# A two-block transformer kernel on one core: throwaway products of TensorE taken out of all its waits but the first

## The chip, the cores and the metric

The kernel runs on one NeuronCore of a Trainium2 chip, in float32. The core has TensorE (matrix products; PE in the profile, with its weight loads apart as PEld), VectorE (DVE), ScalarE (ACT), GpSimd (POOL) and SyncE (SP, which here only starts transfers). They run side by side and wait for each other by semaphores. The metric is the device time of one execution in microseconds (us). Three executions of the kernel before took 2404.06, 2407.88 and 2408.59 us; the median is 2407.88.

## The reference

Two blocks of two layers each work on 256 tokens of 1024 numbers. Cut to what matters here:

```
# first block, for each of 2 layers
h = rms_norm(x, norm_gain[layer]);  proj = h @ w_in[layer]
... sparse attention and a gated delta rule on parts of proj, mixed by gates ...
x = x + mixed @ w_out[layer]
x = rms_norm(x, final_gain)
# second block, for each of 2 layers
a = rms_norm(h, norm_attn[i]);  u = a @ w_in[i]
... four mixers on parts of u ...
h = h + mix @ w_out[i]
c = rms_norm(h, norm_ffn[i])
h = h + (swiglu(c) if i == 0 else moe_swiglu(c))      # moe: top 2 of 8 experts
gate = sigmoid(rms_norm(h, ple_norm[i]) @ ple_w_gate[i])
h = h + (p[i] @ ple_w_proj[i]) * gate
```

The routing of the second layer is

```
logits = x @ router;  top_val, top_idx = top_k(logits, 2);  top_w = softmax(top_val)
out = sum over experts e of combine[:, e] * swiglu_e(x)
```

## The kernel before, in words

The 256 tokens stand as two tiles of 128 partitions. The residual X stays in SBUF, and weights stream in over SyncE's queue into a ring. Every product is in float32, which TensorE runs as two passes: where this text says "three products", the trace counts six.

Before each large product X is normalised. There are nine such norms, n = 0 to 8; norm 2, the end of the first block, is taken together with norm 3. TensorE's part in a norm is `norm_pe`: it turns half of X (four blocks of 128 columns, two token tiles, line 474) into PSUM, from where VectorE writes it, times the gain, to HT (line 597). This is done for the left half of X first, then for the right. A half can be turned once the residual's sum is in X, which VectorE says by `x_updated` (`xf_ready` for norm 3). The left half is often turned in the middle of the last product of the stage before. `norm_rest_pe` (line 660) does the right half, which comes when that product has ended, and so TensorE has nothing of its own to do until VectorE has added the last 512 columns to X.

In this wait the kernel before puts throwaway products. `keep_busy(bank, times)` (line 640) multiplies the identity with one of its own columns, spread to 256, into a PSUM bank that nobody reads then. It waits for nothing but what stands ahead of it in TensorE's order. It is called at twelve places: four products ahead of the first input (line 3626), three in each of the seven `norm_rest_pe` but that of norm 8, three behind `setup_pe`, which turns the small parameters (lines 3419 and 3421) once at the start, four behind the router's logits (line 2862), two ahead of the first experts' gather (line 3038) and two behind it (line 3043).

The order on each engine is the order of the code; where stages overlap, plans written as tables say after how many steps of one another's steps stand. No plan holds a throwaway product.

At the start, the stage is: identity ready; four throwaway products; left half of X turned; three; right half turned; parameters turned; three; then the first product of layer 0 (line 683, lhs HT, first weights in the ring). Its k-th step waits for the k-th block of HT.

In the second layer of the second block the route goes: router logits (line 2859, 32 passes of 8 columns), the top two by VectorE (lines 2875 to 2882), four small products that count places (lines 2864 to 2867), the first experts' places by VectorE (lines 2885 to 2926), the gather of their tokens as products (line 3020, 32 passes), its way out of PSUM by VectorE (line 3232), and then the experts' wide products (line 2968) and down products (line 2981), all eight experts one behind another.

Of the kernel before, what the change touches and what calls it, by code (L numbers as in the profile page):

```python
# [66 lines left out]
def blocks_kernel(nc, A, out):  # L67
    ctx = ExitStack()
    with ctx:
        sems = {}  # L70

        def sem(name):
            if name not in sems:
                sems[name] = ctx.enter_context(nc.semaphore(name))
            return sems[name]
# [20 lines left out]
        def signal(name):  # L96
            return sem(CHAINED[name][0] if name in CHAINED else name)

        def reached(name, times):

            if name in CHAINED:
                _, i, n = CHAINED[name]
                return n * (times - 1) + i + 1
            return times
# [360 lines left out]
        def ht_lhs(k, t):  # L465
            return HT[:, k, t * P:(t + 1) * P]
# [11 lines left out]
        def bc(ap, shape):  # L478
            return ap.to_broadcast(shape)
# [104 lines left out]
        def fresh_from(n):  # L584

            m = turned(n)
            return 2 * KD * min(m, DEPTH) + KD * max(0, m - DEPTH)
# [52 lines left out]
        def keep_busy(bank, times):  # L640

            for _ in range(times):
                nc.tensor.matmul(PS[:, bank, 0:S], IDENT, bc(IDENT[:, 0:1], [P, S]), start=True, stop=True)

        def idle_bank(n):

            return {0: 3, 1: 2, 3: 2}.get(n, 0)

        def norm_pe(pe, n, half):

            if n == DEPTH + 1:
                pe.wait_ge(sem("xf_ready"), half + 1)
                src = XGAIN
            else:
                x_half(pe, n, half)
                src = X
            blocks = [(lambda t, k=k: src[:, t, k * P:(k + 1) * P]) for k in range(4 * half, 4 * half + 4)]
            transposes(blocks, 4 + 2 * half).then_inc(sem("norm_transposed"), 1)

        def norm_rest_pe(pe, n):  # L660
            if n != 8:
                keep_busy(idle_bank(n), 3)
            norm_pe(pe, n, 1)
            if n == 0:
                setup_pe(pe)
                keep_busy(3, 3)

        U = view(0, T * (QKV0)).rearrange("p (t c) -> p t c", t=T)
# [1982 lines left out]
        def ple_turn_pe(pe, L, bank):  # L2652
            pe.wait_ge(sem("ple_loaded"), 16 * (L + 1))
            transposes([(lambda t, j=j: PP[:, t, j * P:(j + 1) * P]) for j in range(2)], bank).then_inc(sem("ple_T"), 1)
# [126 lines left out]
        def half_places(t):  # L2781

            return slice(HALF_CAP * t, HALF_CAP * t + HALF_CAP)
# [12 lines left out]
        def group_places(g, t):  # L2796

            return WSEL[:, t].rearrange("p e s -> p (e s)")[:, g * P:(g + 1) * P]
# [53 lines left out]
        def ms(name):  # L2852
            return sem("moe_" + name)

        def route_pe(pe, n):
            for k in range(KD):
                pe.wait_ge(sem("ht_ready"), fresh_from(n) + (k + 1))
                for t in range(T):
                    last = nc.tensor.matmul(PS[:, 2 * t, 0:NE], ht_lhs(k, t), ROUTER[:, k, :],
                                            start=k == 0, stop=k == KD - 1)  # L2860
            last.then_inc(signal("moe_logits"), 1)
            keep_busy(7, 4)
            pe.wait_ge(signal("moe_mask"), reached("moe_mask", 1))
            nc.tensor.matmul(PS[:, 5, 0:NE], SUPPER, MASK[:, 0, :], start=True, stop=True)
            nc.tensor.matmul(PS[:, 5, NE:2 * NE], SUPPER, MASK[:, 1, :], start=True, stop=True)
            nc.tensor.matmul(PS[:, 5, 2 * NE:3 * NE], ONES, MASK[:, 0, :], start=True, stop=True)
            nc.tensor.matmul(PS[:, 5, 3 * NE:4 * NE], ONES, MASK[:, 1, :], start=True, stop=True)\
                .then_inc(signal("moe_places"), 1)
# [144 lines left out]
        def first_pe(pe):  # L3013

            def gather(i, half):
                for k in range(4 * half, 4 * half + 4):
                    c = k % 2 * 2 * CAP
                    for t in range(T):
                        two = PS[:, (6, 3)[half] + k % 4 // 2, c:c + 2 * CAP].rearrange("p (a s) -> p a s", a=2)
                        last = nc.tensor.matmul(two[:, :, half_places(t)], XN[:, t, k * P:(k + 1) * P],  # L3020
                                                PALL[:, t, 2 * i:2 * i + 2, :], start=True, stop=True)
                last.then_inc(ms("gather"), 1)

            def scatter(i, bank=6):
                g, t = SCATTERS[i]
                for dh in range(2):
                    last = nc.tensor.matmul(PS[:, bank + dh, :], PWG[:, g, t * P:(t + 1) * P],  # L3027
                                            YTG[g % 3][:, 512 * dh:512 * dh + 512], start=True, stop=True)
                last.then_inc(ms("scatter"), 1)

            def weights_turned(g0, g1):
                for g in range(g0, g1):
                    for t in range(T):
                        last = nc.tensor.transpose(PS[:, 6 + (g - g0) // 2, g % 2 * S + t * P:g % 2 * S + (t + 1) * P],
                                                   group_places(g, t), IDENT)
                last.then_inc(ms("placedT"), 1)

            keep_busy(4, 2)
            pe.wait_ge(ms("placed"), 1)
            pe.wait_ge(signal("moe_tokens"), reached("moe_tokens", 1))  # L3040
            gather(0, 0)
            gather(0, 1)
            keep_busy(0, 2)
            for e in range(NE):
                n = SCATTER_AT.get(e)

                def tokens(k, b):
                    c = CAP * (e % 2) + 32 * b
                    return XGP[:, k, c:c + 32]

                if e % 2 == 0:
                    pe.wait_ge(ms("XG"), e + 2)
                wide(pe, 0, e, 0, 0, 3, tokens)
                if e == 0:
                    pe.wait_ge(ms("weighed"), 1)
                    weights_turned(0, 4)
                elif n is not None:
                    pe.wait_ge(ms("YT"), e)
                    if n:
                        pe.wait_ge(ms("added"), n)  # L3060
                    scatter(n)
                wide(pe, 0, e, 0, 3, 6, tokens)
                if n is not None and e % 2:
                    pe.wait_ge(ms("added"), n + 1)
                    scatter(n + 1)
                wide(pe, 0, e, 0, 6, 8, tokens)
                wide(pe, 0, e, 1, 0, 8, tokens)
                if e == 0:
                    pe.wait_ge(ms("PWT"), 1)
                    weights_turned(4, 6)  # L3070
                elif e % 2 == 0 and n is not None:
                    pe.wait_ge(ms("added"), n + 1)
                    scatter(n + 1)
                elif e == 1:
                    pe.wait_ge(ms("PWT"), 2)
                elif n is not None:
                    pe.wait_ge(ms("added"), n + 2)
                if e == NE - 1:
                    ple_turn_pe(pe, 1, 7)
                elif e % 2:  # L3080
                    gather((e + 1) // 2, 0)
                    pe.wait_ge(ms("h"), 2 * e + 2)
                    gather((e + 1) // 2, 1)
                down(pe, 0, e, 0, 24)
                down_last(pe, 0, e)
            pe.wait_ge(sem("ple_pT"), 2)
            ple_unit(pe, 1, 0, 0, 3).then_inc(sem("ple_unit"), 1)
            pe.wait_ge(ms("YT"), NE)
            scatter(len(SCATTERS) - 2)
            scatter(len(SCATTERS) - 1, 4)  # L3090
            ple_unit(pe, 1, 0, 1, 0).then_inc(sem("weights_used"), 1)
# [325 lines left out]
        def setup_pe(pe):  # L3417
            pe.wait_ge(sem("col_params"), 16 * N_COLS)
            nc.tensor.transpose(PS[:, 0, 0:64], PSTAGE[0:64, 0, :], IDENT[0:64, 0:64])
            for L in range(DEPTH):  # L3420
                last = nc.tensor.transpose(PS[:, 0, 64 + 96 * L:160 + 96 * L], PSTAGE[0:96, 1 + L, :],
                                           IDENT[0:96, 0:96])
            last.then_inc(sem("param_cols_T"), 1)
# [266 lines left out]
```

## Time and profile before

| | |
|---|---|
| median of three executions | 2407.88 us |
| the profiled execution, its own time | 2409.21 us |
| span of its trace | 2407.4 us |
| TensorE busy | 2354.6 us, 98% |
| VectorE busy | 821.1 us, 34% |
| ScalarE busy | 462.9 us, 19% |
| transfers | 542.56 MB, mean 225 GB/s |
| experts' stage | 1462 to 2380 us, TensorE busy 914.51 us of 918 |

The profiled execution's own time is 1.8 us above its span; what lies outside the span is ahead of the first and behind the last instruction of the core. It is 1.3 us above the median.
### The profile page before, as it was taken

The numbers are of one execution on the slowest core, as the hardware profiler recorded it, in microseconds if no ns is written. First come the engines' busy times: TensorE is split into PE (matmuls) and PEld (weight loads), VectorE is DVE, ScalarE is ACT, GpSimd is POOL, SyncE is SP. The second block draws the span as 40 slices with busy tenths as digits, with TensorE's granted clock in tenths as the row PEclk, the third lists the DMA queues.
The fourth block names the chain that finished last, engine by engine and source line by source line (L and its number), as shares of the span: only waits on it lengthen the run. The fifth ranks groups of instructions, "written<-read, shape, count | busy, mean of one in ns | idle before, by whom it ended". The sixth has DMA issues, their size and how long they took to land. (4 is left out here: it accounts for less than half of the span.)

```text
span 2407.4 us, 51252 instructions
## 1 busy us (share of the span) xinstructions
PE 2354.6 (98%) x23229; PEld 1364.4 (57%) x23229; DVE 821.1 (34%) x1665; ACT 462.9 (19%) x794; POOL 139.7 (6%) x356
## 2 busy tenths in 40 slices
PE   9999999999999999999999899999999999999999
PEld 8755557855555676997455654435343534343444
DVE  3545623444543554666635531101010101101012
ACT  1532321432323542000025431000000000000001
POOL 5011000011000310000003100000000000000000
PEclk9999999999999999999999999999999999999999
DMA  7522334432335513445446128999999999999992
GB/s 246 168 89 72 122 123 140 137 108 79 104 100 148 176 55 120 154 169 183 158 133 187 52 93 342 397 402 378 405 397 409 379 387 399 369 384 396 388 369 97
DMA packets 194447, 542.56 MB, mean 225 GB/s; under 512 B 29200, under 2 KB 61360, under 8 KB 194224
## 3 DMA queue, kind: packets, MB, share of 16 engines
q1 hardware_dynamic: 180576, 536.82, 60.8%
q8 instruction: 185, 3.03, 0.5%
q10 hardware_dynamic: 13344, 1.35, 0.5%
q0 software_dynamic: 304, 1.05, 0.1%
q14 instruction: 38, 0.31, 0.0%
HBM read 538.12 MB, written 1.05 MB: 224 GB/s over the span
## 5 line engine op out<-in xcount | busy, mean ns | idle before, releaser
L407 PE MATMUL psum<-ring,hT 128*128 128x512 f32 (+3 forms) x1120 | 478.4, 576 | 6.0 <-ACT area L831 4.5
L2968 PE MATMUL psum<-ring,mix 128*32 128x448 f32 x4608 | 438.5, 539 | 0.7 <-DVE mix L3232 0.7
L407 PEld LDWEIGHTS psum<-ring,hT 128*128 128x128 f32 x1120 | 206.0, 190 | 206.4 <-issue 180.9
L2968 PEld LDWEIGHTS psum<-ring,mix 128*32 128x32 f32 x4608 | 148.8, 110 | 282.9 <-issue 280.7
L3221 DVE TENSOR_TENSOR area<-area,psum 128x1344 f32<-128x1344 f32 x16 | 24.6, 1535 | 470.6 <-PE psum L2968 470.6
L712 PE MATMUL psum<-hT,ring 128*128 128x256 f32 x768 | 166.4, 379 | 0.0
L712 PEld LDWEIGHTS psum<-hT,ring 128*128 128x128 f32 x768 | 145.9, 190 | 20.7 <-issue 1.0
L2981 PE MATMUL psum<-area 128*32 128x256 f32 x2688 | 148.2, 379 | 1.9 <-DVE area L3223 1.9
L2968 PE MATMUL psum<-area,mix 128*32 128x448 f32 x1536 | 147.2, 539 | 0.0
L2981 PE MATMUL psum<-ring,area 128*32 128x256 f32 x2688 | 146.5, 379 | 0.0
L2981 PEld LDWEIGHTS psum<-area 128*32 128x32 f32 x2688 | 86.5, 110 | 61.4 <-DVE area L3223 3.2
L2981 PEld LDWEIGHTS psum<-ring,area 128*32 128x32 f32 x2688 | 87.3, 110 | 57.8
L3165 ACT ACTIVATE area<-psum 128x256 f32<-128x256 f32 x24 | 9.2, 384 | 512.1 <-PE psum L2981 512.1
L1699 PE MATMUL psum<-ring,hT 128*128 128x256 f32 x384 | 102.8, 413 | 1.2 <-ACT area L1627 1.2
L2968 PEld LDWEIGHTS psum<-area,mix 128*32 128x32 f32 x1536 | 49.9, 110 | 94.4 <-issue 94.4
L3259 DVE COPY hT<-area 32x256 f32<-32x256 f32 x64 | 18.2, 285 | 223.6 <-ACT area L3165 222.9
L1699 PEld LDWEIGHTS psum<-ring,hT 128*128 128x128 f32 x384 | 73.4, 202 | 19.0 <-issue 5.7
L3157 ACT ACTIVATE area<-psum 128x1344 f32<-128x1344 f32 x16 | 20.7, 1291 | 272.2 <-PE psum L2968 272.2
L2446 PE MATMUL psum<-area 128*128 128x128 f32 x576 | 66.3, 275 | 0.0
L2446 PEld LDWEIGHTS psum<-area 128*128 128x128 f32 x576 | 65.3, 192 | 0.0
L1517 PE MATMUL psum<-ring,hT 128*128 128x512 f32 x128 | 59.5, 623 | 4.0 <-issue 4.0
L920 DVE SCALAR_TENSOR_TENSOR area<-area,param_cols 128x256 f32<-128x256 f32 x144 | 60.5, 482 | 1.3
(592 smaller groups left out, 2581.5 us busy)
## 6 DMA issues: line engine op xcount, KB each, us to landing
ring<-in_w_in_dram SPq DMA_DIRECT2D x88, 1024.0 KB, 5.1
ring<-in_moe_w_gate_dram SPq DMA_DIRECT2D x96, 896.0 KB, 7.0
ring<-in_moe_w_up_dram SPq DMA_DIRECT2D x96, 896.0 KB, 8.0
area<-in_moe_w_down_dram SPq DMA_DIRECT2D x112, 512.0 KB, 5.9
ring<-in_moe_w_down_dram SPq DMA_DIRECT2D x112, 512.0 KB, 6.5
area<-in_moe_w_gate_dram SPq DMA_DIRECT2D x32, 896.0 KB, 7.3
area<-in_moe_w_up_dram SPq DMA_DIRECT2D x32, 896.0 KB, 7.6
ring<-in_w_out_dram SPq DMA_DIRECT2D x16, 1024.0 KB, 5.0
```

Of the source, the lines that this page charges most:

```text
L407: last = nc.tensor.matmul(acc(g)[:, t, 0:d["n"]], lhs(kk, t), w[:, k, :], start=kk == 0, stop=kk == d["nk"] - 1)
L712: last = nc.tensor.matmul(acc(g)[:, j // 2, (j % 2) * S:(j % 2) * S + S], half_view(n, (4, 512))[:, k % 4, j * P:(j + 1) * P], HT[:, k, :] ...
L920: ins = nc.vector.scalar_tensor_tensor(Y[:, c, :], XC[:, c, tap:tap + S], w, Y[:, c, :], ALU.mult, ALU.add)
L1517: last = nc.tensor.matmul(acc(g)[:, t, :], mixed(k)[:, 4 * h + kk, t * P:(t + 1) * P], w[:, kk, :], start=h + kk == 0, stop=h == 1 and kk ...
L1699: last = nc.tensor.matmul(acc(g)[:, t, :], ht_lhs(k, t), w[:, k, :], start=k == 0, stop=k == KD - 1)
L2446: last = nc.tensor.matmul(out[:, j, :], w[:, k, j * P:(j + 1) * P], h[:, k, :], start=k == 0, stop=k == 3)
L2968: last = nc.tensor.matmul(PS[32 * j:32 * j + 32, 3 * p + b, 0:PIECE].rearrange("p (m n) -> p m n", n=32), tokens(k, b), w[:, :, j, :], sta ...
L2981: return nc.tensor.matmul(PS[32 * jj:32 * jj + 32, b, 0:256], HET[:, i // 14, b, 32 * (i % 14):32 * (i % 14) + 32], ring_cols(chunk_place( ...
L3157: nc.scalar.activation(HE[:, p], PS[:, 3 * p:3 * p + 3, 0:PIECE], ACT.Silu).then_inc(ms("sg"), 1)
L3165: nc.scalar.activation(YE[:, b, :], PS[:, b, 0:256], ACT.Copy).then_inc(ms("YE"), 1)
L3221: nc.vector.tensor_tensor(HE[:, p], HE[:, p], PS[:, 3 * p:3 * p + 3, 0:PIECE], ALU.mult).then_inc(ms("h"), 1)
L3259: ins = nc.vector.tensor_copy(YTG[g % 3][r0:r0 + 32, 256 * j:256 * j + 256], YE[32 * j:32 * j + 32, b, :])
```

## The change

All calls of `keep_busy` are taken out but the one ahead of the first input (line 3626). Thirty-two products, 64 passes, go from eleven places. No other instruction is added or moved; a semaphore wait that stood on a throwaway product goes to the instruction behind it.

```diff
         def norm_rest_pe(pe, n):
-            if n != 8:
-                keep_busy(idle_bank(n), 3)
             norm_pe(pe, n, 1)
             if n == 0:
                 setup_pe(pe)
-                keep_busy(3, 3)
...
             last.then_inc(signal("moe_logits"), 1)
-            keep_busy(7, 4)
             pe.wait_ge(signal("moe_mask"), reached("moe_mask", 1))
...
-            keep_busy(4, 2)
             pe.wait_ge(ms("placed"), 1)
             pe.wait_ge(signal("moe_tokens"), reached("moe_tokens", 1))
             gather(0, 0)
             gather(0, 1)
-            keep_busy(0, 2)
             for e in range(NE):
```

TensorE's order around norm 5, the one ahead of the gate product of the second block's first layer, before (L474 turns the right half of X, L2666 are the products of the per-layer input, L407 is the gate product):

```order
L2666 MATMUL psum<-ring,area 128x512 [waits landed0,ple_pT]
L2666 MATMUL psum<-ring,area 128x512
L643 MATMUL psum<-ident 128x256 [waits ple_out_dve]
L643 MATMUL psum<-ident 128x256 x2
L474 MATMUL psum<-ident,x 128x128 [waits x_updated]
L474 MATMUL psum<-ident,x 128x128 x7
L2666 MATMUL psum<-ring,area 128x512 [waits landed0]
L2666 MATMUL psum<-ring,area 128x512
L407 MATMUL psum<-ring,hT 128x512 [waits ht_ready,landed1,x_updated]
```

The same place now (the lines have moved by three):

```order
L2663 MATMUL psum<-ring,area 128x512 [waits landed0,ple_pT]
L2663 MATMUL psum<-ring,area 128x512
L474 MATMUL psum<-ident,x 128x128 [waits x_updated,ple_out_dve]
L474 MATMUL psum<-ident,x 128x128 x7
L2663 MATMUL psum<-ring,area 128x512 [waits landed0]
L2663 MATMUL psum<-ring,area 128x512
L407 MATMUL psum<-ring,hT 128x512 [waits ht_ready,landed1,x_updated]
```

The wait for `ple_out_dve`, VectorE's copy of the first of these products, stood on the first throwaway product and stands on the turning now.

TensorE's order from the end of the router's logits to the first expert, before (the small products are L2864 to L2867, the gather is L3020, the first expert L2968):

```order
L2859 MATMUL psum<-router,hT 128x8
L643 MATMUL psum<-ident 128x256 x4
L2864 MATMUL psum<-area,supper 128x8 [waits route_by_vector]
L2865 MATMUL psum<-area,supper 128x8
L2866 MATMUL psum<-area,ones 128x8
L2867 MATMUL psum<-area,ones 128x8
L643 MATMUL psum<-ident 128x256 x2
L3020 MATMUL psum<-area,xn 128x2x48 [waits route_by_scalar,moe_placed]
L3020 MATMUL psum<-area,xn 128x2x48 x15
L643 MATMUL psum<-ident 128x256 x2
L2968 MATMUL psum<-ring,mix 32x448 [waits moe_landed1,moe_XG]
```

And now:

```order
L2856 MATMUL psum<-router,hT 128x8
L2860 MATMUL psum<-area,supper 128x8 [waits route_by_vector]
L2861 MATMUL psum<-area,supper 128x8
L2862 MATMUL psum<-area,ones 128x8
L2863 MATMUL psum<-area,ones 128x8
L3016 MATMUL psum<-area,xn 128x2x48 [waits route_by_scalar,moe_placed]
L3016 MATMUL psum<-area,xn 128x2x48 x15
L2964 MATMUL psum<-ring,mix 32x448 [waits moe_landed1,moe_XG]
```

Eight products are gone from three waits that lie within ten microseconds; the real products stand as they stood.

## Rows read from the trace of the kernel before

**Rows 1.** The page, the chain that ended last, shares of the span by line.
```profile
PE psum L2968 23%; PE psum L2981 12%; PE psum L1517 1%; PE psum L1699 1%; PE psum L3027 1%; DVE area L3221 1%; PE psum L407 1%; PE psum L2690 1%; PE psum L474 0%; ACT area L2027 0%; PE psum L2666 0%; PE psum L2012 0%; PE psum L3020 0%; DVE area L3223 0%; PE psum L1988 0%
```

**Rows 2.** Timeline of TensorE, norm 5: start us, us, what, idle before it.
```profile
1214.93 1.57 PE L643 MATMUL psum<-ident 128*128 128x256 f32 x6 [0.85 <-DVE mix L2643]
1216.34 1.03 PE L474 MATMUL psum<-ident,x 128*128 128x128 f32 x8
```

**Rows 3.** Timeline of VectorE and of TensorE, norm 6.
```profile
1250.83 0.69 DVE L2729 TENSOR_TENSOR x<-x,area 128x512 f32<-128x512 f32 x1
...
1252.02 1.04 PE L474 MATMUL psum<-ident,x 128*128 128x128 f32 x8
```

**Rows 4.** Timeline of TensorE, norm 1, whose wait is that of norms 4 and 7.
```profile
374.13 3.60 PE L1517 MATMUL psum<-ring,area 128*128 128x512 f32 x8
...
379.12 1.09 PE L474 MATMUL psum<-ident,x 128*128 128x128 f32 x8
```

**Rows 5.** Timeline of TensorE, norm 3.
```profile
747.97 1.47 PE L643 MATMUL psum<-ident 128*128 128x256 f32 x6
750.78 1.09 PE L474 MATMUL psum<-ident,mix 128*128 128x128 f32 x8 [1.34 <-DVE mix L551]
```

**Rows 6.** Timeline of TensorE, the start.
```profile
6.60 1.47 PE L643 MATMUL psum<-ident 128*128 128x256 f32 x6
7.91 1.04 PE L474 MATMUL psum<-ident,x 128*128 128x128 f32 x8
9.15 0.27 PE L3419 MATMUL psum<-ident,area 64*128 64x64 f32 x1 [0.20 <-DMA area<-in_conv_w_dram]
...
9.57 1.50 PE L643 MATMUL psum<-ident 128*128 128x256 f32 x6
11.60 4.56 PE L683 MATMUL psum<-ring,hT 128*128 128x256 f32 x20 [0.53 <-DVE hT L597]
16.07 0.71 PE L688 MATMUL psum<-ident,small 128*128 128x128 f32 x4
```

**Rows 7.** Timeline of TensorE, and of VectorE at 1459.60, the route.
```profile
1448.21 3.64 PE L2859 MATMUL psum<-router,hT 128*128 128x8 f32 x32
...
1453.89 0.39 PE L2864 MATMUL psum<-area,supper 128*128 128x8 f32 x2 [0.20 <-DVE area L2882]
...
1454.81 1.11 PE L643 MATMUL psum<-ident 128*128 128x256 f32 x4
1456.09 3.81 PE L3020 MATMUL psum<-area,xn 128*128 128x96 f32 x32 [0.16 <-DVE area L2926]
...
1459.60 1.82 DVE L3232 TENSOR_TENSOR mix<-psum,param_cols 128x768 f32<-128x768 f32 x2
...
1461.48 0.96 PE L2968 MATMUL psum<-ring,mix 128*32 128x448 f32 x8 [0.69 <-DVE mix L3232]
```

**Rows 8.** Timeline of TensorE, waits without throwaway products elsewhere.
```profile
841.44 1.14 PE L1988 MATMUL psum<-area 64*128 64x256 f32 x8 [1.59 <-DVE mix L1926]
...
861.40 1.93 PE L2012 MATMUL psum<-area 128*32 128x64 f32 x64 [2.12 <-ACT area L2035]
...
910.46 8.80 PE L1517 MATMUL psum<-ring,hT 128*128 128x512 f32 x16 [1.99 <-issue]
...
1338.61 1.09 PE L2001 MATMUL psum<-ident,area 128*128 128x128 f32 x8 [2.75 <-ACT area L2027]
```

**Rows 9.** Stretches behind those waits: engines' busy us, granted clock (PEclk), transfers.
```profile
841.40:844.90 3.50, 3.46 (x77) 2.62 (x78) 2.15 (x2) 0.61 (x2) 0.00 (x0) 1.00 0.02 5
859.70:866.40 6.70, 5.00 (x71) 4.22 (x72) 2.94 (x8) 3.36 (x8) 4.66 (x10) 0.50 0.03 8
910.80:914.20 3.40, 3.40 (x5) 1.35 (x4) 1.59 (x3) 1.07 (x2) 0.00 (x0) 0.50 0.00 0
1340.90:1344.30 3.40, 2.67 (x7) 1.59 (x5) 2.19 (x4) 2.80 (x4) 0.00 (x0) 0.50 0.00 0
```

**Rows 10.** Timeline of TensorE, the same 64 passes as at 861.40, at full clock.
```profile
1346.59 1.10 PE L2012 MATMUL psum<-area 128*32 128x64 f32 x64
```

## The prediction

> **What bounds the kernel now.** I read the page first. The chain that ended last runs nearly wholly over TensorE's products [rows 1], those of the experts ahead of all, and TensorE has no long pause in any slice. A microsecond won or lost on TensorE ahead of the experts therefore goes to the end, where nothing else covers it. The second view is the timeline at the eleven places. For each the question is what ended the wait in which the throwaway products stood. If real work behind them started when they ended, they delayed it. If it started later, with idle time of its own, taking them out wins nothing, and the wait is then wholly idle. The third view is the granted clock behind such idle waits elsewhere in this trace. A product at 1.2 GHz takes twice its time, and this is what the change can cost.
>
> **What is won.** A throwaway set of three products is six passes. Six take 1.47 us with a tail of 0.16 [rows 5], so they stand 0.215 us apart and hold TensorE for 1.3 us.
>
> Norm 5: the throwaway passes start at 1214.93, where VectorE's copy ends, and the turning starts at 1216.34, with no idle time between [rows 2]. The right half of X had long been there, since VectorE adds it ahead of that copy. Now the turning starts at 1214.93. A turning that was waited for takes 1.09 us against 1.04 for one that was not [rows 4, 2], so the gain is 1216.34 - 1214.93 - 0.05 = 1.36 us. Behind it stand real products that wait for nothing late; the gate product needs the right half's first block of HT only after its first sixteen passes. All 1.36 us should come through.
>
> Norm 6: VectorE's sum of the right half ends at 1250.83 + 0.69 = 1251.52, and the turning starts at 1252.02 [rows 3]. With 0.04 us for the semaphore it could start at 1251.56. The gain is 0.46, less the same 0.05: 0.4 us.
>
> Norms 1, 4 and 7 look alike: the real product ends at 374.13 + 3.60 = 377.73, and the turning starts at 379.12, after the throwaway passes, when VectorE's sum has ended [rows 4]. Nothing is won, and the idle wait is 1.39 us. Norm 3: the turning waits 1.34 us beyond the throwaway passes for VectorE [rows 5]. Nothing is won.
>
> The start: the right half is turned at 7.91, and could be at about 6.6. But the parameters that are turned next are waited for until 9.15, by a transfer, and the first product at 11.60 waits for VectorE's HT, which hangs on the parameters [rows 6]. Nothing is won. The route: the small products wait for VectorE at 1453.89, the gather for VectorE at 1456.09, the first expert for VectorE at 1461.48, each with idle time of its own [rows 7]. Nothing is won by the eight products there.
>
> The sum of gains is 1.36 + 0.4 = 1.8 us. It could be 1.3 if norm 6 gives nothing and 2.0 at most; nothing else of the 64 passes stands in the way of work.
>
> **What it can cost.** The trace shows four idle waits of TensorE without throwaway products. Behind 1.59 us at 841.44 the clock stays at 1.00. Behind 2.12, 1.99 and 2.75 us it goes to 0.50, for 6.7 us once and 3.4 us twice [rows 8, 9]. Each wait of the changed kernel is set beside the nearest of these four. The price: 16 wide passes behind the wait at 910.46 take 8.80 us [rows 8]. Eight at full clock take 3.60 [rows 4], so 16 take 2 x 3.44 + 0.16 = 7.04. One fall onto wide products costs 1.76 us. Small passes lose too: the same 64 take 1.93 us at half clock and 1.10 at full [rows 8, 10], a factor of 1.75.
>
> Now the waits as they become.
>
> Norms 1, 4, 7: 1.39 us idle with dense work on both sides. Shorter than 1.59, so no fall: 0. The other end is 1.76 each.
>
> Norm 3: the last real pass ends about 747.97 + 0.16, the turning starts at 750.78 [rows 5]: 2.65 us idle. By the row of 2.75 it falls. The half stretch may begin during the wait, and then part of it lies on nothing. Between 0 and 1.76; I take 1.2, since it may also not fall at all in some executions.
>
> The start: the right half's turning would end at about 7.6, then 1.5 us idle until 9.15, half a microsecond of small turnings, whose tail ends at 9.57 + 0.16 = 9.73, and from there to 11.60 idle again, 1.87 us [rows 6]. The two together are longer than any of the waits that fell. The half clock then lies on the first product, whose 20 passes run from 11.60; they end at 11.60 + 20 x 0.215 = 15.9, and the next group waits for VectorE until 16.07, which covers 0.17. One stretch of 3.4 us costs up to 1.76 - 0.17 = 1.6, and one of 6.7 us, as at 859.70, 3.2. The least is 0. I take 1.3.
>
> The route: from the logits' end at 1448.21 + 3.64 = 1451.85 to 1453.89 TensorE idles 2.04 us; then eight small passes until 1454.81 + 0.16 = 1454.97, and 1.12 us idle to the gather at 1456.09 [rows 7]. A fall is nearly certain. It lies on the eight small passes (1.08 us, at 1.75 times 0.8 more) and on the gather (3.81 us, up to 2.9 more). A stretch of 3.4 us wholly on the gather loses 3.4 x (1 - 1/1.75) = 1.45. VectorE's second instruction of L3232 starts at 1459.60 + 0.91 = 1460.51 [rows 7], 0.6 us after the gather's end, and covers so much: 0.85 left. One that begins at the small passes gives 0.8 + 0.2. A long stretch gives up to 2.4. Between 0 and 2.4; I take 1.2.
>
> The first expert: 1459.90 to 1461.48, 1.58 us idle behind a gather of light passes [rows 7]. It is just at the row that held, so a fall is as likely not: between 0 and 1.76; I take 0.4.
>
> The sum: -1.8 + 1.3 + 1.2 + 1.2 + 0.4 = +2.3 us. On the profiled execution's own 2409.21 that is 2411.5. This execution is 1.3 us above the median of the runs, so for the median I forecast 2410.2.
>
> The ends: all gains and no fall gives -1.8 to -2.0. All falls at their dearest gives 3.2 + 1.76 + 2.4 + 1.76 - 1.8 = +7.3, and three more at the quiet norms +12.6.
>
> **A rule that speaks against the change.** The trace shows turnings at full clock: eight passes in 1.04 us [rows 2, 3, 6]. Whether the chip counts them as work when it decides on the clock, no row here says alone. The Trainium skill, "TensorE: Matmul & The Clock Gate", section "Part 4: PE-mode transpose", says that the full clock "doesn't engage" for transposes, since they don't count as busy in the same way. By this the pause at norms 1, 4 and 7 would be longer for the chip than the 1.39 us of the row, and these would fall too. It is the second rival.
>
> **The rivals.** A change within 0.2% (4.8 us) is what a measurement of this kernel can't tell from none; the three runs spread over 4.5 us.
>
> First rival: the clock does not fall at the new waits, because the work around them is denser than around those that fell. For it: 1.59 us held, and each of norms 1, 4, 7 is shorter. Against it: norm 3's 2.65 us and the two pairs at the start and in the route are as long as those that fell or longer. Then only the gains stay: 2407.88 - 1.8 = 2406.1. Chance 0.17.
>
> Second rival: turnings don't hold the clock, and norms 1, 4 and 7 fall too. A turning's 0.9 us adds to 1.39 and makes 2.3 us, beyond the 1.99 that fell. The stretch lies on the wide product behind, 1.3 to 1.76 us each, so 4 to 5.3 more: 2414.2 to 2415.5. For it: nothing in the rows excludes it. Against it: the wait before 841.44 is as long as these and held, though no turning stands beside it. Chance 0.1.
>
> Third rival, the slower one: the half clock lasts a second stretch, because what stands behind the wait is itself sparse. The places are the start, where the first product is only begun when the stretch is half over, and the route, where small passes and another wait follow. The row of 6.7 us at 0.50 shows that it happens: its work was sparse, busy 5.00 us of it by a view that counts tails [rows 9]. Price: 3.2 at the start and 2.4 in the route in place of 1.3 and 1.2, with norm 3 and the first expert at 1.76: +7.3, so 2415.2. It decides the sign of the measurement from a total loss of 6.6 us on. Chance 0.23.
>
> The forecast keeps 0.5: two to four falls of single stretches, 2407.5 to 2413.
>
> **How the numbers follow.** Slower by over 0.2% is above 2412.7: a tenth of the forecast's 0.5, most of the second rival and nearly all of the third, 0.05 + 0.08 + 0.2 = 0.33. Faster by over 0.2% is below 2403.1, for which no term is large enough; 0.04 is left for the spread of the runs beside the first rival. Within 0.2% is the rest, 0.63. The range is 2405.5 to 2416: it takes in the first rival and the third, and leaves out the second at full price.
>
> **What would show it.** The turning at norm 5 starts right at VectorE's copy, 1.4 us earlier against its neighbours; at norm 6 it starts at VectorE's sum. The waits at norms 1, 3, 4 and 7 end where they end now. The granted clock stands at 0.50 behind norm 3, in the first 16 us and between 1453 and 1461, and the first product's 20 passes take 5 to 6 us in place of 4.56. If the clock is 1.00 there, the first rival holds; if 0.50 stands behind norms 1, 4 and 7, the second; if it lasts more than 4 us at the start or in the route, the third. The forecast is wrong if the experts' stage changes in length, since no term of it touches that.

## The result, and the profile after

The changed kernel takes 2414.61 us in the median of 16 executions (2406.24 to 2425.01), the kernel before 2409.66 in 16 (2404.06 to 2412.72). The ratio is 1.0024, with a 95% interval of 1.0013 to 1.0036: 3 to 9 us slower. The forecast was 2410.2, with 2405.5 to 2416 as its range and +2.3 us as its sum, and it gave a time within 0.2% the larger chance, 0.63 against 0.33 for slower; what came lies just outside. The sign was right, and the size was half of what came. The losses stand at the places named, and at one more that the forecast did not have.

The profiled execution of the changed kernel took 2410.15 us, the second fastest of its sixteen. So the two traces can't be set against each other by their ends, only place by place. Between the places both kernels have stretches in which the clock falls in one execution and not in the next. From 380 to 743 us, for one, the two traces drift by 2.5 us against each other, with no changed instruction there.

In the trace before, the clock stood at 1.00 at the start, at norm 3 and in the route. The rows are stretches: engines' busy us (PE, PEld, DVE, ACT, POOL), then the granted clock, the share of the transfers and GB/s.

```profile
9.70:13.12 3.42, 2.89 (x14) 2.25 (x13) 3.24 (x8) 0.00 (x0) 3.15 (x5) 1.00 0.98 334
13.12:16.53 3.41, 3.41 (x19) 2.78 (x18) 2.40 (x9) 0.20 (x1) 2.84 (x10) 1.00 1.05 399
...
750.39:753.81 3.42, 3.03 (x18) 2.68 (x19) 2.82 (x8) 1.36 (x4) 0.00 (x0) 1.00 0.51 172
...
1446.00:1462.00 16.00, 14.87 (x110) 12.65 (x112) 11.77 (x41) 4.72 (x7) 0.75 (x1) 1.00 0.90 361
```

The same places in the changed kernel, with norms 1 and 4. They answer to [rows 9], which had only waits elsewhere.

```profile
11.30:18.10 6.80, 5.72 (x14) 4.59 (x15) 5.03 (x15) 0.20 (x1) 5.78 (x17) 0.50 1.04 389
...
383.00:386.40 3.40, 3.17 (x19) 2.92 (x20) 2.77 (x9) 0.72 (x2) 0.00 (x0) 1.00 0.86 304
...
752.10:755.40 3.30, 3.02 (x11) 2.78 (x12) 1.86 (x6) 1.26 (x4) 0.00 (x0) 0.50 0.45 153
...
945.00:948.40 3.40, 3.20 (x19) 2.95 (x20) 2.77 (x9) 0.72 (x2) 0.77 (x1) 1.00 0.99 347
...
1448.40:1458.50 10.10, 7.13 (x33) 7.04 (x33) 6.76 (x30) 2.94 (x4) 0.00 (x0) 0.50 0.94 389
```

The reader is to see the clock column: 1.2 GHz at the start for 6.8 us, behind norm 3 for 3.4, and in the route for 10.1. Behind norms 1 (383) and 4 (945) it stays at 2.4 GHz.

What it did to the work stands in the timeline of TensorE, the start first. It answers to [rows 6].

```profile
6.76 1.09 PE L474 MATMUL psum<-ident,x 128*128 128x128 f32 x8 [0.35 <-DMA x<-in_x_dram]
9.93 0.27 PE L3413 MATMUL psum<-ident,area 64*128 64x64 f32 x1 [2.07 <-DMA area<-in_conv_w_dram]
...
12.38 7.40 PE L680 MATMUL psum<-ring,hT 128*128 128x256 f32 x20 [1.86 <-DVE hT L597]
19.61 0.61 PE L685 MATMUL psum<-ident,small 128*128 128x128 f32 x4
```

The 20 passes of the first product take 7.40 us, where they took 4.56. The parameters' transfer also landed later, at 9.93 instead of 9.15; that has nothing to do with the change, as the traces of the kernels below show, where the first product starts 0.3 to 1.3 us later than in the trace before, with and without the throwaway products at the start. From the first pass of this product to the first of the next one (line 709, 712 before) it is 2.66 us more.

Norms 3, 5 and 6, which answer to [rows 5], [rows 2] and [rows 3], in the timeline of TensorE:

```profile
752.38 1.97 PE L474 MATMUL psum<-ident,mix 128*128 128x128 f32 x8 [2.64 <-DVE mix L551]
...
1215.45 1.09 PE L474 MATMUL psum<-ident,x 128*128 128x128 f32 x8 [0.85 <-DVE mix L2640]
...
1250.74 1.09 PE L474 MATMUL psum<-ident,x 128*128 128x128 f32 x8 [0.70 <-DVE x L2726]
```

At norm 3 even the turning runs at half clock, 1.97 us instead of 1.09. At norms 5 and 6 the turning follows VectorE at once.

The route, which answers to [rows 7]:

```profile
1443.62 1.09 PE L474 MATMUL psum<-ident,x 128*128 128x128 f32 x8 [1.38 <-DVE x L1548]
1444.55 3.64 PE L2856 MATMUL psum<-router,hT 128*128 128x8 f32 x32
1450.23 0.60 PE L2860 MATMUL psum<-area,supper 128*128 128x8 f32 x2 [2.04 <-DVE area L2878]
...
1453.25 6.34 PE L3016 MATMUL psum<-area,xn 128*128 128x96 f32 x32 [1.14 <-DVE area L2922]
1460.63 1.71 PE L2964 MATMUL psum<-ring,mix 128*32 128x448 f32 x16 [1.05 <-DVE mix L3226]
```

The gather takes 6.34 us instead of 3.81. The clock fell at 1448.33, when the logits had only just ended at 1448.19 (1444.55 + 3.64): the passes of 8 columns had kept TensorE at work until then, with no pause since 1443.62.

The experts' stage, which the prediction named as the part that must not change, did not: from its first pass to the first of the four products ahead of norm 8's turning it is 908.05 us before and 908.04 now.

Behind it, at norm 8, stands one thing that no term of the sum had. No throwaway product ever stood there:

```profile
2370.51 0.87 PE L474 MATMUL psum<-ident,x 128*128 128x128 f32 x6
2372.89 1.31 PE L474 MATMUL psum<-ident,x 128*128 128x128 f32 x10 [1.51 <-issue]
```

The same in the trace of the kernel before:

```profile
2371.36 1.97 PE L474 MATMUL psum<-ident,x 128*128 128x128 f32 x16
```

After six of sixteen passes TensorE stands for 1.51 us, and the profile shows nothing that it waits for (`issue`).

### The profile page after: what moved, and what is told of

Read it like the earlier page. It is cut to its first block, busy times and chain, and to the rows that moved or that the text cites. A ratio compares the mean times of both kernels' runs of the same rounds, so it can differ in the third digit from the quotient of the medians.

```text
span 2408.3 us, 51125 instructions
## 1 busy us (share of the span) xinstructions
PE 2341.5 (97%) x23165; PEld 1356.5 (56%) x23165; DVE 820.9 (34%) x1665; ACT 462.9 (19%) x794; POOL 138.4 (6%) x356
## 3 DMA queue, kind: packets, MB, share of 16 engines
q10 hardware_dynamic: 13344, 1.35, 0.5%
## 4 chain that ended last, share of the span: by engine, by line
PE 61%; DVE 2%; issue 1%; ACT 1%; DVEq 0%; ACTq 0%
PE psum L2964 23%; PE psum L2977 12%; PE psum L2443 6%; PE psum L407 4%; PE psum L2478 3%; PE psum L1696 3%; PE psum L1514 2%; PE psum L2424 1%; PE psum L3023 1%; PE psum L474 1%; DVE area L3215 1%; PE psum L2687 1%; PE psum L2663 1%; PE psum L3016 1%; PE psum L2259 0%
## 5 line engine op out<-in xcount | busy, mean ns | idle before, releaser
L407 PE MATMUL psum<-ring,hT 128*128 128x512 f32 (+3 forms) x1120 | 477.6, 575 | 7.0 <-ACT area L828 4.5
L407 PEld LDWEIGHTS psum<-ring,hT 128*128 128x128 f32 x1120 | 206.3, 191 | 207.6 <-issue 182.0
```

What stands on the lines that cost most here:

```text
L407: last = nc.tensor.matmul(acc(g)[:, t, 0:d["n"]], lhs(kk, t), w[:, k, :], start=kk == 0, stop=kk == d["nk"] - 1)
```

## The experiments

All kernels are the kernel before with the edits shown, cut to what matters. Behind each stand the medians of its executions and of the kernel before beside it, and the ratio on record with its 95% interval. That ratio is not the quotient of the two medians and lies up to 0.0008 from it. The table gives what a place costs in each trace: the start of a pass behind the place minus the start of a pass ahead of it, less the same in the trace before (the starts as the timelines have them). The places are the start (first pass of the first product to the first of the next), norm 3 (743 to 756 us), norms 5 and 6 (1209 to 1218.9, and 1249.8 to 1257), the route (first pass of the logits to the experts' first) and norm 8 (2369.5 to 2374.9).

| kernel | start | norm 3 | norm 5 | norm 6 | route | norm 8 |
|---|---|---|---|---|---|---|
| changed | +2.66 | +1.46 | -1.35 | -0.38 | +2.81 | +1.73 |
| changed, again | +2.09 | +1.67 | -1.35 | -0.39 | +4.30 | +1.82 |
| e8_after147 | +1.85 | +1.67 | -1.35 | -0.39 | +3.05 | 0 |
| e1_start | +2.58 | 0 | 0 | 0 | 0 | 0 |
| e2_norm3 | +0.11 | +1.68 | 0 | 0 | +1.87 | 0 |
| e3_route | +0.10 | 0 | 0 | 0 | +2.86 | 0 |
| e4_norm56 | +0.10 | 0 | -1.35 | -0.38 | 0 | 0 |
| e5_norm147 | +0.12 | 0 | 0 | 0 | +2.83 | 0 |
| e7_mix | +0.11 | 0 | -1.35 | -0.38 | +3.52 | 0 |
| e10_mix_ffn | +0.11 | 0 | -1.35 | -0.39 | +1.86 | 0 |
| e11_light | +1.89 | 0 | 0 | 0 | +3.52 | 0 |
| e12_light_again | +1.50 | 0 | 0 | 0 | +3.52 | 0 |
| e13_light_third | +1.46 | 0 | 0 | 0 | +3.52 | 0 |

**e1_start: the start alone.**

```diff
         def norm_rest_pe(pe, n):
-            if n != 8:
+            if n in (1, 3, 4, 5, 6, 7):
                 keep_busy(idle_bank(n), 3)
...
                 setup_pe(pe)
-                keep_busy(3, 3)
```

> Only the six products at the start are taken out (three ahead of the right half's turning in norm 0, three behind the parameters). Clock theory: the granted clock falls to 0.50 ahead of or in the first product of layer 0, and stays there for 3.4 or 6.8 us; the first product's 20 passes take 6 to 8 us in place of 4.56, and the run is 1.5 to 3.3 us slower than before. Rival (the cost is code placement: TensorE stood 1.5 us for no shown reason in the turning of norm 8 in the changed kernel): the start costs nothing, and the time follows whether that stop appears in norm 8.

Measured: 2409.0 us against 2406.91, ratio 1.0008 (0.9996 to 1.0020), not told from no change by its time. The trace shows the mechanism, timeline and clock:

```profile
11.99 7.33 PE L682 MATMUL psum<-ring,hT 128*128 128x256 f32 x20 [1.86 <-DVE hT L597]
```

```profile
10.90:17.60 6.70, 5.61 (x13) 4.55 (x14) 5.03 (x15) 0.20 (x1) 5.63 (x18) 0.50 1.05 389
```

6.8 us at half clock again, 2.58 us lost. The code placement rival is out for this place: the loss is there, and norm 8 is unchanged.

**e2_norm3: norm 3 alone.** `if n in (0, 1, 4, 5, 6, 7):` ahead of the call.

> Only the three products ahead of norm 3's right half are taken out. Clock theory: 0.50 for 3.4 us around the turning or the product behind it, 1.0 to 1.7 us slower than before. Rival (code placement): clock and time as before at norm 3; any loss shows as a stop of TensorE in norm 8.

Measured: 2406.04 against 2406.91, ratio 1.0001 (0.9990 to 1.0013): the loss of 1.0 to 1.7 us is not to be seen in the times. In the trace norm 3 costs 1.68 us:

```profile
749.40:752.70 3.30, 3.30 (x9) 2.34 (x9) 2.69 (x11) 0.21 (x1) 0.00 (x0) 0.50 0.00 0
1445.70:1452.40 6.70, 6.70 (x25) 5.88 (x24) 3.84 (x21) 2.46 (x3) 0.00 (x0) 0.50 1.02 428
```

The second row is a surprise: the clock fell in the route too, with all its throwaway products in place.

**e3_route: the route alone.** The three calls `keep_busy(7, 4)`, `keep_busy(4, 2)` and `keep_busy(0, 2)` are out.

> Only the eight products of the route are taken out (behind the logits, ahead of and behind the first gather). Clock theory: the clock falls in the route, and the stretch from the logits' end to the first expert's first wide pass grows by 2 to 3.5 us over the 9.6 us of before; the run is 2 to 3.5 us slower. Rival (code placement): this stretch grows by less than 0.5 us.

Measured: 2409.31 against 2406.91, ratio 1.0007 (0.9994 to 1.0020), not told from no change. In the trace the route costs 2.86 us, with 10.2 us at half clock:

```profile
1441.40:1451.50 10.10, 7.28 (x33) 7.19 (x34) 6.61 (x30) 2.78 (x4) 0.00 (x0) 0.50 0.91 381
```

**e4_norm56: norms 5 and 6 alone.** `if n in (0, 1, 3, 4, 7):` ahead of the call.

> Only the products ahead of the right halves of norms 5 and 6 are taken out. Here they delayed work: the turning of norm 5 should start at VectorE's copy, 1.4 us earlier, and that of norm 6 0.4 us earlier, with the clock at 1.00 there; 1.8 us faster than before. Rival (the clock falls here too): 0 to 1.5 us slower.

Measured: 2403.26 against 2406.91, ratio 0.9986 (0.9975 to 0.9997): faster. The two gains are there to a tenth, 1.35 and 0.38 us, and the clock stays up at both:

```profile
1213.36 1.09 PE L474 MATMUL psum<-ident,x 128*128 128x128 f32 x8 [0.85 <-DVE mix L2643]
...
1248.65 1.09 PE L474 MATMUL psum<-ident,x 128*128 128x128 f32 x8 [0.70 <-DVE x L2729]
```

```profile
1209.00:1218.00 9.00, 8.15 (x31) 4.37 (x31) 6.41 (x16) 2.85 (x8) 0.00 (x0) 1.00 0.52 137
1244.00:1254.00 10.00, 9.30 (x44) 6.60 (x43) 7.27 (x17) 4.97 (x11) 0.00 (x0) 1.00 0.59 186
```

**e5_norm147: norms 1, 4 and 7 alone.** `if n in (0, 3, 5, 6):` ahead of the call.

> Only the products ahead of the right halves of norms 1, 4 and 7 are taken out, where the waits become 1.4 us of idle time. Theory: each of the three turnings starts where it did, the clock stays at 1.00 behind norms 1 and 4, and the run is within 1 us of before; at norm 7 the logits with their light passes follow, and the clock may fall there more often than before. Rival (turnings don't hold the clock): 0.50 behind norms 1 and 4 too, 1.3 to 1.8 us each, 4 to 5 us slower in all.

Measured: 2407.99 against 2406.09, ratio 1.0000 (0.9990 to 1.0010). Norms 1 and 4 cost nothing, and the clock is at 1.00 behind both, so the rival is refuted there. Norm 7 is another matter: the clock fell in the logits behind it.

```profile
1444.86 1.09 PE L474 MATMUL psum<-ident,x 128*128 128x128 f32 x8 [1.38 <-DVE x L1551]
1445.79 5.39 PE L2859 MATMUL psum<-router,hT 128*128 128x8 f32 x32
1451.04 3.53 PE L643 MATMUL psum<-ident 128*128 128x256 f32 x8
```

The logits take 5.39 us instead of 3.64, and the route costs 2.83. This is one trace. In e7_mix below the clock fell in the logits too, with norm 7's products in place.

**e8_after147: the changed kernel with norms 1, 4 and 7 put back.** `if n in (1, 4, 7): keep_busy(idle_bank(n), 3)`, all other calls as in the changed kernel.

> The changed kernel with the three products of norms 1, 4 and 7 put back, 36 instructions of TensorE more than the changed kernel and 92 fewer than before, all ahead of the branch behind the experts. Code placement theory: the stop of 1.5 us in the turning of norm 8 goes away, and the run is 1 to 2 us faster than the changed kernel, 3 to 4 slower than before. Rival (the stop belongs to something else, or to chance): it stays or varies, and the time is that of the changed kernel.

Measured: 2412.46 against 2406.09, ratio 1.0020 (1.0010 to 1.0031). The stop in norm 8 is gone:

```profile
2375.74 1.97 PE L474 MATMUL psum<-ident,x 128*128 128x128 f32 x16
```

The other places cost about what they cost in the changed kernel. But the times do not show the 1 to 2 us that were expected back: 1.0020 (1.0010 to 1.0031) here and 1.0024 (1.0013 to 1.0036) for the changed kernel are not told apart.

**The changed kernel again.**

> The changed kernel once more. Code placement theory: the stop of 1.5 us in the turning of norm 8, after its first six passes, stands in this trace at the same pass. The clock falls again at the start, at norm 3 and in the route, the lengths of the stretches can differ. Chance theory: the stop is gone or elsewhere.

Measured: one execution, 2412.14 us. The stop is there, at the same pass (the view ends at 2376 us):

```profile
2372.51 0.88 PE L474 MATMUL psum<-ident,x 128*128 128x128 f32 x6
2374.99 1.20 PE L474 MATMUL psum<-ident,x 128*128 128x128 f32 x9 [1.60 <-issue]
```

The clock fell at all three places again, in the route for 13.7 us (4.30 us lost).

**e7_mix: norms 5 and 6 out, and throwaway products where the clock fell before.**

```diff
             gemm_begin(pe, left)
+            if k >= DEPTH:
+                keep_busy(TILES[left]["bank"], 4)
             pe.wait_ge(sem("mixT_ready"), 2 * k + 1)
```

> The products ahead of norms 5 and 6 are taken out, as in e4_norm56, and four products each are put into the two waits of TensorE between the turning of the first half of the mixers' output and the output product (2 us of idle time, in both layers of the second block), into the bank that the product fills next. Theory: the clock no longer falls at about 910 and 1410 us, each of which costs up to 1.76 us in the executions where it falls; 0.5 to 3 us faster than e4_norm56, 3 to 6 us faster than before. Rival (the throwaway products delay the product, or the fall comes elsewhere): as e4_norm56 or slower.

Measured: 2401.46 against 2406.09 in seven executions, ratio 0.9977 (0.9963 to 0.9990): faster than the kernel before. From e4_norm56, with 0.9986 (0.9975 to 0.9997), it is not told apart by its time. The output product's 16 passes, 8.80 us in [rows 8], take 7.13 in both layers:

```profile
910.82 1.91 PE L643 MATMUL psum<-ident 128*128 128x256 f32 x8
912.93 7.13 PE L1517 MATMUL psum<-ring,hT 128*128 128x512 f32 x16 [0.20 <-ACT hT L1543]
```

At these two waits the clock fell behind 14 of 24 in the twelve traces without products there, and behind none of the four in this trace and e10_mix_ffn's.

In this trace, too, the clock fell in the route, for 10.2 us, in spite of the products there. It fell at 1442.42, in the middle of the logits, which started at 1439.53 and take 4.20 us; ahead of them norm 7's products and turning stand with no pause.

**e10_mix_ffn: one more place.** As e7_mix, with `keep_busy(7, 4)` ahead of `ple_turn_pe(pe, L, 7)` in the dense layer.

> e7_mix, and four more throwaway products in the dense layer's down product, ahead of the turning of the per-layer input, where TensorE then waits 2.2 us for VectorE's sums (the clock fell there, at about 1197 us, in most traces). Theory: no fall there, 1 to 1.8 us less in the executions where it fell: 0 to 1.8 us faster than e7_mix. Rival (the four products hold up the turning, whose output is needed later): as e7_mix or up to 1.7 us slower.

Measured: 2403.38 against 2407.65, ratio 0.9978 (0.9964 to 0.9992). The clock doesn't fall at 1197 us, but it didn't there in e7_mix either, nor in e3_route and the changed kernel, which have no products there. So one trace doesn't show that the products did it, and by its time the kernel is not told apart from e7_mix.

**e11_light: light throwaway products at the start and in the route.** In short (the line `keep_light(3, 6)` stands twice in the kernel, ahead of norm 0's turning and behind `setup_pe`):

```diff
+        def keep_light(bank, times):
+            for _ in range(times):
+                nc.tensor.matmul(PS[:, bank, 0:8], IDENT, bc(IDENT[:, 0:1], [P, 8]), start=True, stop=True)
...
-                keep_busy(3, 3)
+                keep_light(3, 6)
...
-            keep_busy(7, 4)
+            keep_light(7, 8)
...
-            keep_busy(4, 2)
+            keep_light(4, 4)
...
-            keep_busy(0, 2)
+            keep_light(0, 4)
```

> The products at the start and in the route stand where they stood, but are of 8 columns in place of 256, and twice as many: 6, 6, 8, 4 and 4 products of about 0.22 us each, so that TensorE is as long at work by the trace. Theory A (the kind of work counts, as the fall during the router's 8-column logits suggests): the clock falls at the start and in the route as if nothing stood there; first weights' product 20 passes in 6 to 7.4 us, route 2 to 3 us longer, run 4 to 6 us slower than before. Theory B (being busy is enough): no fall at the start, and the time of before within 1 us.

> The kernel of e11_light once more, for a second trace. In its first trace the clock fell at the start and in the route, but that execution was the slowest of its ten. If passes of 8 columns don't hold the clock (theory A), it falls at both places again: 0.50 in the first product of layer 0, whose 20 passes take 6 us or more, and in the route. If it depends on the execution (theory C), one of the two is at 1.00, with 4.56 us for the 20 passes.

> The same kernel a third time, the same question: theory A has the clock fall at both places again, theory C at one or none.

The clock fell at both places in all three traces. The first one's, stretches and timeline:

```profile
10.30:17.00 6.70, 6.70 (x24) 5.89 (x23) 5.85 (x15) 0.20 (x1) 5.81 (x15) 0.50 1.01 373
1454.20:1464.30 10.10, 10.10 (x49) 10.10 (x49) 6.15 (x27) 2.24 (x3) 0.00 (x0) 0.50 0.85 358
```

```profile
10.38 2.62 PE L648 MATMUL psum<-ident 128*128 128x8 f32 x12
12.85 6.63 PE L690 MATMUL psum<-ring,hT 128*128 128x256 f32 x20
```

TensorE is busy for all of the 10.10 us, and stands at half clock. The start decides between the theories: with products of 256 columns there the clock fell in none of seven traces, with products of 8 columns in three of three. The route alone would not, since the clock fell there in three of six traces with the wide products too.

But by its times the kernel is not 4 to 6 us slower: 2408.46 against 2407.65 in ten executions, ratio 1.0000 (0.9986 to 1.0014), at most 3.4 us. Their mean granted clock is lower, 0.9893 against 0.9908. The three traced executions took 2414.20, 2416.94 and 2412.58. Theory A holds for what the traces show; why the timed executions lose less stays open.

## Why the prediction was right or wrong

**What is won.** Right, in place and size: 1.36 and 0.4 us forecast, 1.35 and 0.38 measured in each of five kernels without these products. Nothing was won anywhere else.

**Norms 1 and 4.** Right: 1.38 us idle, clock at 1.00, nothing lost. The second rival, that turnings don't hold the clock, is refuted for these two places, in the three traces in which their products are out. The Trainium skill's sentence in "TensorE: Matmul & The Clock Gate", section "Part 4: PE-mode transpose", by which they would have fallen, is not borne out here: 1.38 us of idle time and 0.9 us of turning, and 1.00 behind them.

**Norm 3.** The mechanism was right (2.65 us idle forecast, 2.64 measured), and the term a little small: 1.2 forecast, 1.46 to 1.68 in four traces of four. I had marked it down for executions in which it does not fall, and there was none.

**The start.** This is the term that was mis-sized most against its own words: 1.3 forecast, 1.85 to 2.66 measured in the four traces without the products. The clock stayed at half for 6.8 us each time. The third rival had this, with 3.2 us as its price and a chance of 0.23. By the prediction's own signs (more than 4 us at half clock at the start or in the route) it is the third rival that came. That the measured 2414.61 lies so near its 2415.2 is luck in part: the kernel before took 1.8 us more here than in the three executions that I had (2409.66 against 2407.88), and as a difference +4.95 lies halfway between the forecast's +2.3 and the rival's +7.3. I had priced the typical case by the 3.4 us stretches that were the more frequent elsewhere.

What goes with the length can be read from the seven traces in which it fell at the start. In the five where the half clock began 1.0 us or more ahead of the first product of layer 0, it lasted 6.8 us. In e12_light_again's and e13_light_third's it began within 0.5 us of that product's start, and lasted 3.4; these cost 1.50 and 1.46 us. Why it is so no run here shows.

**The route and the first expert.** 1.2 + 0.4 forecast, 2.8 to 4.3 measured in the four traces without the eight products. Two steps failed. One is a sum: by the prediction's own prices the dearest case of the route is 0.8 for the small passes and 2.9 for the gather, less the 0.6 that VectorE covers, so 3.1, where 2.4 is written; in the changed kernel the small passes lost 0.82 and the gather and its way out 1.99.

The other is the idle time as the only measure. I had counted the wait from 1451.85 and taken the logits ahead of it as work. The clock fell with the logits' last pass in the changed kernel, in the middle of them in its second trace and in e5_norm147, where TensorE had not paused since the turning, and in e7_mix, where it had not paused since 1424.59. So the wait isn't needed for the fall. In the changed kernel the clock was back at 1458.57, in the last passes of the gather. The first expert itself ran at full clock.

The trace of the kernel before had shown this already, at a place that the prediction did not look at. Here TensorE runs mostly passes of 32 to 128 columns (lines 2235 to 2271), busy for all of 3.42 us, and then the clock falls:

```profile
822.07:825.49 3.42, 3.42 (x172) 2.84 (x171) 2.81 (x5) 0.53 (x2) 2.79 (x8) 1.00 0.31 116
825.49:828.90 3.41, 3.26 (x12) 2.61 (x11) 1.27 (x3) 0.81 (x3) 0.00 (x0) 0.50 0.02 5
```

That trace has twelve falls ahead of the experts, and not three, and more waits than the four of [rows 8]: 1.69 us at 1312.18 and 1.77 at 579.45, both next to narrow passes, have a fall 1.4 and 0.3 us behind their end, though they are hardly longer than the 1.59 that held.

Norm 7 is open. I had put it at 0, because its wait is like those of norms 1 and 4, but the logits stand behind it. In the one trace with its products alone taken out, e5_norm147's, the route costs 2.83 us. With them in place it costs up to 3.52 in other traces, and e5_norm147's times are those of the kernel before (1.0000, 0.9990 to 1.0010). So no run shows that norm 7's products are worth anything, nor that they aren't.

The kernel before pays part of this too. In six traces that have all products of norm 7 and of the route in place, those of the kernel before, e1_start, e2_norm3, e4_norm56, e7_mix and e10_mix_ffn, the route costs 0, 0, 1.87, 0, 3.52 and 1.86 us: 1.2 in the mean. Without the eight products it costs 2.81, 4.30, 3.05 and 2.86, 3.3 in the mean. So the change costs about 2 us there rather than 3.

**Norm 8.** Not in the prediction: 1.73 and 1.82 us. Of the eleven different kernels traced, only the changed one has the stop, in both of its traces at the same pass; with 36 instructions put back ahead of it, it is gone. What stands close ahead is the branch that skips the passes for overflowing experts. I take it for the loading of code behind a taken branch, with a border of what is loaded at one time shifted to the seventh pass by the instructions taken out. The Trainium skill, "Runtime: NRT & Kernel Launch", section "Instruction fetch mechanics", says that code is loaded in blocks ahead of the sequencer, and that a taken branch to code that isn't loaded makes the engine wait for it. The trace agrees so far that it shows a stop with no releaser there.

It shows more in the transfers. TensorE has such stops (`issue`, over 1 us) in the trace before too, 2.32 us at 527.01 and 1.69 at 1312.18, and they stand elsewhere in other kernels. Leaving out the 1.99 us ahead of the two products of [rows 8], each of them in the traces ends 2.2 to 2.8 us after a packet of 16384 bytes has started on the instruction queue q8, and so do the two at norm 8: the packet starts at 2370.52 and the turning goes on at 2372.89, and 2372.44 and 2374.99 in the second trace. All such idle time together, without the very short pauses, is 6.8 us before, 9.1 and 8.5 in the two traces of the changed kernel and 7.5 in e8_after147's. That the stop at norm 8 comes and goes with instructions far ahead is shown, in two traces with it and one of e8_after147 without it; that it is the loading fits every stop, and is argued all the same, since no view shows what code is loaded when.

**The sum.** The row "changed" of the table gives 2.66 + 1.46 + 2.81 + 1.73 - 1.35 - 0.38 = +6.9 us. Less the 1.2 that the kernel before pays in the route, this makes +5.7. Measured are +4.95 in the medians, with 3 to 9 as its interval. Forecast were +2.3. Of the table's sum the forecast lacks 3.4 us: the start (+1.4), norm 3 (+0.3) and norm 8 (+1.7), while the route's overrun (1.2) and what before pays there cancel.

The runs' own clocks say nearly the same without any trace. Each execution has its mean granted clock beside its time. Over 82 executions of the kernel before, the time falls by 1.9 us for each 0.001 that the mean clock rises (0.001 of 2407 us is 4.8 us at half clock, so about 40% of such a stretch is lost). They have 0.9910 and 2406.98 us in the mean; the changed kernel's sixteen have 0.9871 and 2414.94. Eight of the sixteen lie below 0.988, the lowest of the 82, and for these the line is drawn on. Brought to the clock of before, the changed kernel has 2407.5. What is left is half a microsecond, give or take 1.4 (95%, from the spread of the executions): most of the loss is the clock, and the gains of 1.7 and the stop of 1.7 would cancel. The same reckoning has e4_norm56, which has the gains alone, 2.6 us (give or take 1.1) below the kernel before. But it has e8_after147, with the gains and without the stop, at 0.1 below (give or take 1.4), where 1.7 were to be expected. So the stop's share is read from the traces, and the times don't bear it out.

## What to carry to other kernels

Price throwaway products place by place. Where their end is followed at once by real work, they delay it, and out they go (0.14% here). Where the wait ends later than they do, they cost nothing, and they are worth the fall that they prevent, if there is one: 1.5 to 2.7 us at norm 3 and the start, about 2 in the route, nothing at norms 1 and 4. They can be tried where the clock falls in the trace and none stood; e7_mix is 0.23% faster than before, but 0.14% came with norms 5 and 6 alone, and the rest is not told from nothing. Read the granted clock over the whole trace, not only behind idle waits, and look at narrow passes next to a wait with the same doubt as at the wait.

## What the runs showed of the hardware that I had not expected

The clock fell from 2.4 to 1.2 GHz while TensorE ran passes of 8 columns without a pause, during the logits in e5_norm147 and e7_mix. In the route of e11_light TensorE was busy for all of 10.1 us and stood at 1.2 GHz, and so in all three traces of that kernel. In the route half clock lasted 6.8 to 13.7 us, behind norm 3, where wide passes follow, 3.4 us.

Taking out instructions far ahead can open a stop of 1.5 us in code that was not touched. Stops of this kind end 2.2 to 2.8 us after the start of a packet on the instruction queue.

The times of one kernel spread over 14 us (2399.67 to 2414.20 for the kernel before in 35 executions), and the mean granted clock accounts for most of it (71% of the variance of the 82). A difference of 2 us, as in e1_start, was plain in a trace and not to be seen in twelve times.
